# Hybrid encoder trunk: early loads at the FFN entry, and three layer boundaries interleaved by input chunk

## The chip, the cores and the metric

The kernel runs on one core of one Trainium2 chip (trn2). The metric is the device time of one execution in microseconds (us); lower is better. The profile is one execution's, taken by the hardware profiler.

## The reference

Two layers over a sequence of 256 tokens of width 2048, all float32. Each half of a layer is a sandwich of RMS norms around a matrix chain:

```
for layer in range(2):
    h = rms_norm(x, norm_mix_pre[layer])
    m = even_mixer(h, ...) if layer == 0 else diff_attention_mixer(h, ...)
    x = x + rms_norm(m, norm_mix_post[layer])
    h = rms_norm(x, norm_ffn_pre[layer])
    f = (silu(h @ w_gate) * (h @ w_up)) @ w_down          # 2048 -> 5632 -> 2048
    x = x + rms_norm(f, norm_ffn_post[layer])
```

The mixers are one input projection (2048 to 5120 in layer 0, 2048 to 6144 in layer 1), recurrence and attention, and one output projection (2048 to 2048).

## The kernel before, in words

**Products.** Every weight matrix is cut into 512x512 pieces of 1 MB, the "units" u = 0, 1, 2 ... in the order of use. SP loads a piece into a raw buffer (L775). ACT writes its float32r rounding, `w_hi` (L909, task `hi`). DVE writes the remainder, `w_lo = raw - w_hi` (L1499, task `lo`), which also sets the raw buffer free. PE multiplies in three passes, w_hi with the high part of the activations, w_lo with the high part, w_hi with their low part (L1241), for 128 tokens at a time: a `half(slot, t)` is 12 matmuls, t is 0 or 1. There are four `w_hi` buffers and three `w_lo` buffers, so `hi(u)` waits until PE has done unit u-4 and `lo(u)` until it has done u-3. There are five raw buffers. Three (`raw`) serve the mixers and boundaries; two more (`gx`, `queries`) belong to the attention and serve as raw buffers 3 and 4 in the FFN blocks only.

**Order.** Nothing is scheduled at run time. One list of tasks per part is written out beforehand and every engine goes through it in order, doing its own share of each task and waiting on semaphores. So a task that waits holds back all that stands behind it on its engine.

**Boundaries.** Between two matrix chains (b=1: mixer output of layer 0 to FFN of layer 0, b=2: FFN of layer 0 to mixer of layer 1, b=3: mixer to FFN of layer 1) stands `boundary(b, before, after)`, an order written out by hand. `before` are the last four units (column groups s0 to s3 of the old output); for each column group and token half there are: add_output (DVE L1579), y_square (ACT L925), rms_y (DVE, then POOL), y_gain (POOL or DVE L1571), update of the residual (DVE L1562), `turn` (four PE transposes L1264, then high part by ACT L955 and low part by DVE L1537), square (ACT L925). When all squares of the new residual are there, rms_x gives the scale of the next norm (POOL). `after` are the first four units of the next chain, e, f, g, h: one column group over the four 512-wide chunks of the input, chunk by chunk. `head_end` lists the rest of the FFN's head.

**FFN.** The first 512 of the 5632 columns are the "head": four gate units, then four up units, silu (ACT L1107) and gate_up (DVE L1773). The other ten pieces of columns are "blocks" (class Body). A block saves matmuls: the products of the 2x2 corner of input chunks 0 and 1, token halves 0 and 1, gate and up, are made from seven products (P1 to P7) of sums and differences of weights and activations instead of eight. `ENTRIES` is the order of PE, `LOADS` that of SP. P1 needs g0; P5 the difference u0-g0, formed on DVE in g0's buffer (L1512); P3 needs u1; P6 u1 minus that difference (L1514), P7 u1-u0 (L1517), P4 g1 minus what g0's buffer then holds (L1519). The activations' sums S1 to S4 ("left sums") are made once per layer: eight additions on POOL (L1980 to L1996), then high parts (ACT L1118) and low parts (DVE L1528). P5 needs S1, P3 needs S4. The blocks' products P1 to P7 are at L1254. After P5, PE transposes gate_up's result for the down products.

**Buffers of the loads.** `place_loads` goes through the loads in SP's order and gives each the buffer whose last load is oldest by a number `age`; the load waits until what was in that buffer is released. In a block u1's buffer is released by form P7, u0's by lo P7, g0's by lo P4, g2's by lo g2, g1's by form P4. In the kernel before, the block's loads are u1, u0, g0, g2, g1, and then u3 takes u1's buffer, g3 u0's, u2 g0's, and so on in rotation. Ahead of the first block SP issues the gain vector of the next norm, 1 MB as it lands (L817), then these loads.

The DVE's order in a block, which the prediction follows, begins:

```
form(body, "P6"); low("P3"); low("P6"); low("g2"); form(body, "P7"); second()
low("P2"); form(body, "P4"); low("P7"); low("P4"); low("u3"); third()
```

Of the kernel before, what the change touches and what calls it, by code (L numbers as in the profile page):

```python
# [59 lines left out]
KEYS_SLOT = ((20, 31), (4,))  # L60
# [38 lines left out]
LOADS = ("u1", "u0", "g0", "g2", "g1", "u3", "g3", "u2", "d0", "d1", "d3", "d2")  # L99
FORMS = ("P5", "P6", "P7", "P4")  # L100
# [4 lines left out]
class Body:  # L105


    def __init__(self, layer, j, index, u, n, e, m, n_head):

        self.layer, self.j, self.index, self.first = layer, j, index, j == 0  # L110
        self.base, self.e, self.m = u, e, m
        self.u = {name: u + i for i, name in enumerate(ENTRIES)}
        self.up, self.gate, self.down = n, n + 1, n + 2
        self.head_up, self.next = n_head + 1, None
        self.form = {name: len(FORMS) * index + i + 1 for i, name in enumerate(FORMS)}
        self.sum = {name: len(SUMS) * index + i + 1 for i, name in enumerate(SUMS)}

# [39 lines left out]
def mixer_slots(plan, layer):  # L157
# [7 lines left out]
    if layer == 0:  # L165
        order = ([("xr", g, 2 + g) for g in range(2)] + [("gate", g, g) for g in range(2)]
                 + [(w, g, 4 + 2 * i + g) for g in range(2) for i, w in enumerate("qkv")])
        groups, w_in, w_out = 2, "ev_in", "ev_out"
    else:
        order = [(w, g, 4 * i + g) for g in range(4) for i, w in enumerate("qkv")]  # L170
        groups, w_in, w_out = 4, "od_in", "od_out"
# [6 lines left out]
    if layer == 0:  # L178
        for kg in range(NC):
            for _, g, cb in order[:2]:  # L180
                slots.append(plan.slot(w_in, kg, plan.n + g, kg == 0, kg == NC - 1, cb=cb, region="h", layer=layer))
        plan.n += 2
    for i, (what, g, cb) in enumerate(order):
        if layer == 0 and i < 2:
# [25 lines left out]
    starts = [evacs["v", g].s + 1 + 2 * (layer == 0 and g == 0) for g in range(groups)]  # L210
    for s in range(len(slots)):
        for kind, lag in (("s0", 0), ("pt", 1), ("pv", 2), ("s", 0)):
            for g, start in enumerate(starts):
                i = s - start - lag
                if 0 <= i < HEADS_OF_GROUP:
                    task = put(s, kind=kind, g=g, i=i, n=plan.heads + HEADS_OF_GROUP * g + i, v_group=evacs["v", g].n)
                    if kind == "pt" and layer == 1:
                        slots[s].early.append(Task("difference", n=task.n))
# [75 lines left out]
def head_end(slots, body):  # L294

    def left(name):
        return Task("sums", 2 * body.layer + 1, body.layer, what=name)

    tasks = []
    for i, s in enumerate(slots):  # L300
        last = len(slots) - 1 - i
        tasks += half(s, 0)
        tasks += [hi(u) for u in range(ahead(s.u - 1, HI_LEAD), min(ahead(s.u, HI_LEAD), body.base + 1))]
        tasks += [lo(u) for u in range(ahead(s.u - 1, LO_LEAD), min(ahead(s.u, LO_LEAD), body.base + 1))]
        if last == 1:
            tasks += [Task("form", src=body, what="P5"), hi(body.base + 1), lo(body.base + 1)]
        if last == 0:
            tasks += [left("S1"), left("S3")]
        tasks += half(s, 1) + s.post
    return tasks + [left("S2"), left("S4")]  # L310
# [35 lines left out]
def boundary(b, before, after):  # L346


    update, turn, square = boundary_tasks(b)
    add, y_square, rms_y, y_gain = y_tasks(b)  # L350
    s0, s1, s2, s3 = before
    e, f, g, h = after
    u = s0.u
    tasks = [hi(u + 3)] + half(s0, 0) + [lo(u + 2)] + half(s1, 0) + half(s0, 1, [add(s1, 0), add(s0, 0)])
    tasks += [hi(u + 4), y_square(s1, 0)] + half(s2, 0, [lo(u + 3)]) + [add(s2, 0), y_square(s0, 0), add(s0, 1)]
    tasks += half(s1, 1) + half(s3, 0)
    tasks += [add(s1, 1), lo(u + 4), y_square(s2, 0), y_gain(1, 0), y_square(s0, 1), add(s3, 0), y_square(s1, 1), y_gain(0, 0), y_gain(1, 1, "dve"), y_gain(0, 1, "dve")]
    tasks += half(s2, 1, [y_square(s3, 0)]) + [rms_y(0), add(s2, 1), update(0, 0), hi(u + 5), y_square(s2, 1)]
    tasks += half(s3, 1)
    tasks += [update(1, 0), lo(u + 5), add(s3, 1), turn(0, 0), y_square(s3, 1), y_gain(2, 1), y_gain(2, 0), rms_y(1), turn(1, 0)]  # L360
    tasks += half(e, 0)
    tasks += half(f, 0, [update(0, 1), update(2, 0), hi(u + 6)], [y_gain(3, 0, "dve"), update(1, 1), turn(0, 1), square(0, 0)])
    tasks += [turn(1, 1)] + half(e, 1, [square(1, 1)])
    tasks += [update(2, 1), lo(u + 6), update(3, 0), hi(u + 7), y_gain(3, 1, "dve"), turn(2, 0), turn(2, 1), update(3, 1)]
    tasks += half(f, 1, [square(2, 0), lo(u + 7), square(2, 1)], [hi(u + 8)]) + half(g, 0, [square(1, 0)])
    tasks += [turn(3, 0), square(3, 0)] + half(g, 1)
    tasks += [turn(3, 1), square(0, 1), hi(u + 9), square(3, 1), hi(u + 10)] + half(h, 0) + [lo(u + 8)]
    tasks += half(h, 1, [Task("rms_x", b), *h.post]) + [lo(u + 9)]
    return tasks
# [82 lines left out]
def make_plan():  # L452
    plan, before = Plan(), None
    for layer in range(2):
# [4 lines left out]
                for w, n in (("gate", n_gate), ("up", n_up)) for kg in range(NC)]  # L459
# [3 lines left out]
        head[NC - 1].post.append(Task("silu", 2 * layer + 1, n=n_gate, u=head[NC - 1].u))  # L463
# [8 lines left out]
        n_start = NC if before else 2 * NC  # L472
        start = boundary(2 * layer, before, slots[:NC]) if before else first_boundary(slots[:n_start])
        tasks = (start + run(slots[n_start:-NC]) + boundary(2 * layer + 1, slots[-NC:], head[:NC]) + head_end(head[NC:], bodies[0]))
# [30 lines left out]
def place_loads(plan):  # L505
# [4 lines left out]
    def take(key, buffers, released):  # L510
# [6 lines left out]
        age[buf] = BLOCK_RAW + order  # L517

    age[3:] = [-2, -1]
    for part in plan.parts:  # L520
        for task in part.tasks or ():
            if task.kind == "tile_unit" or task.kind == "half" and task.t == 0 and task.passes[0] == 0:
                take(task.slot.u, range(RAW), (("lo", task.slot.u + 1),))
        for body in part.bodies or ():
            lo_of = {name: ("lo", u + 1) for name, u in body.u.items()}
            form_of = {name: ("form", n) for name, n in body.form.items()}
            released = {"g0": (lo_of["P4"],), "u0": (lo_of["P7"],), "u1": (lo_of["P3"], form_of["P7"]),
                        "g1": (lo_of["P2"], form_of["P4"])}
            for name in LOADS:
                take((body.index, name), range(BLOCK_RAW), released.get(name) or (lo_of[name],))  # L530
# [7 lines left out]
def trunk(nc, x, norm_mix_pre, norm_mix_post, norm_ffn_pre, norm_ffn_post,  # L538
# [9 lines left out]
    with ExitStack() as ctx:  # L548
# [215 lines left out]
        def _(sp):  # L764
# [53 lines left out]

            def load_slot(slot):
# [8 lines left out]
            def task_of(task):  # L828
                if task.kind == "tile_unit" or task.kind == "half" and task.t == 0 and task.passes[0] == 0:
                    load_slot(task.slot)  # L830
                elif task.kind == "gains":
# [22 lines left out]
            for part in plan.parts:  # L854
# [4 lines left out]
                wg, wu, wd = (weights[w][part.layer] for w in ("gate", "up", "down"))  # L859

                def block_load(body, name):

                    cols, rows = slice((body.j + 1) * KC, (body.j + 2) * KC), slice(body.j * KC, (body.j + 1) * KC)
                    k = int(name[1])
                    if name[0] == "d":
                        src = wd[rows, k * KC:(k + 1) * KC]
                    else:
                        src = (wg if name[0] == "g" else wu)[k * KC:(k + 1) * KC, cols]
                    load((body.index, name), src)

                sp.wait_ge(s_done, plan.heads_of[part.layer])
                for body in part.bodies:
                    for name in LOADS:
# [324 lines left out]
        def _(pe):  # L1198
# [59 lines left out]

            def transposes(e, pieces):
# [10 lines left out]
            def task_of(task):  # L1270
# [13 lines left out]
                elif task.kind == "T":  # L1284
# [19 lines left out]
                    else:  # L1304
                        transposes(task.e, quarter(task.e, src, task.t))
                elif task.kind == "tile_unit":
# [71 lines left out]
            for part in plan.parts:  # L1378
# [10 lines left out]
                def rows(kg, t):  # L1389
                    return [b[:, kg * KT:(kg + 1) * KT, t * P:(t + 1) * P] for b in (h_hi, h_lo)]  # L1390

# [25 lines left out]

                def down(body, j):
# [5 lines left out]
                def block(body):  # L1424
# [10 lines left out]
                    for name in ENTRIES:  # L1435
                        if name == "P1":
                            if not body.first:
                                pe.wait_ge(copied[0], body.index)
                            formed(body, name, product1, rows(0, 0), True, True)
# [612 lines left out]
```

## Time and profile before

| | us |
|---|---|
| median of 3 runs | 2233.23 |
| lowest, highest | 2232.08, 2234.36 |
| profiled execution, its time | 2234.35 |
| its span in the trace | 2232.6 |
| PE busy in it | 2202.4 (99%) |
| DVE, ACT, POOL busy | 1688.6, 1176.9, 309.9 |
| mean granted TensorE clock | 0.997 |

PE is TensorE's matmul side, PEld its weight loads, DVE VectorE, ACT ScalarE, POOL GpSimd, SP the engine that issues the transfers. The times of a timeline count from the start of the span. A busy PE is a stretch covered by matmuls; what it is short of the span is time in which no matmul ran. "<- X" names what released a waiting instruction. The three boundaries lie around 356 to 410, 1071 to 1125 and 1486 to 1540 us. The first blocks of the two layers begin at 427 and 1557 us.

### The profile page before, as it was taken

What the parts mean: (1) busy time and instruction counts of PE and PEld (TensorE: products, weight loads), DVE (VectorE), ACT (ScalarE), POOL (GpSimd) and SP (SyncE); (2) the same over time, 40 slices, a digit from 0 to 9 for tenths busy, and PEclk for the clock granted to TensorE, in tenths of its full rate; (3) what the DMA queues carried; (4) which work ended last, traced back from release to release, by engine and by line L of the source; (5) the groups of instructions that cost most, each with busy time, mean ns of one, the idle gap of its engine ahead of it and who ended that gap; (6) DMA issues with size and microseconds to landing.
All of it is one profiled execution on the core that took longest, in us unless ns stands there. A gap on an engine that the chain in (4) does not pass through costs nothing.

```text
span 2232.6 us, 26301 instructions
## 1 busy us (share of the span) xinstructions
PE 2202.4 (99%) x10011; PEld 1812.0 (81%) x10011; DVE 1688.6 (76%) x1680; ACT 1176.9 (53%) x1330; POOL 309.9 (14%) x253
## 2 busy tenths in 40 slices
PE   8999999999999999999999999999999999999998
PEld 6888888788888888888787888787788888888886
DVE  5587467788888888888746555777888888888886
ACT  6677545545554444454655555546454444444543
POOL 0851001200000000000121001003000000000001
PEclk9999999999999999999999999999999999999999
DMA  8545444466564445664564545455565445565543
GB/s 306 184 162 172 167 132 151 170 226 226 189 225 174 172 171 205 222 226 152 177 214 137 170 151 169 170 169 191 196 219 186 173 171 204 208 226 204 211 170 113
DMA packets 213883, 416.52 MB, mean 187 GB/s; under 512 B 12328, under 2 KB 14976, under 8 KB 213248
## 3 DMA queue, kind: packets, MB, share of 16 engines
q1 hardware_dynamic: 213040, 414.29, 53.0%
q8 instruction: 81, 1.33, 0.2%
q10 hardware_dynamic: 720, 0.56, 0.1%
q14 instruction: 42, 0.34, 0.0%
HBM read 412.73 MB, written 2.10 MB: 186 GB/s over the span
## 4 chain that ended last, share of the span: by engine, by line
PE 92%; DVE 3%; DMA 2%; issue 1%; ACT 1%; SPq 1%; ACTq 0%; POOLq 0%; POOL 0%; DVEq 0%
PE acc L1241 69%; PE acc L1254 12%; PE tp L1264 2%; PE sc L1254 2%; PE pv L1254 2%; DMA raw<-in_ffn_w_gate 1%; PE sc L1344 1%; DVE w_lo L1499 1%; PE pv L1373 1%; PE sc L1340 1%; DMA raw<-in_ev_w_in 1%; PE pv L1368 1%; ACT w_hi L909 0%; DMA yacc<-in_x_T 0%; PE sc L1323 0%
## 5 line engine op out<-in xcount | busy, mean ns | idle before, releaser
L909 ACT ACTIVATE w_hi<-raw 128x2048 fp32r<-128x2048 f32 x321 | 612.9, 1915 | 454.8 <-DVE raw L1512 93.4
L1499 DVE TENSOR_TENSOR w_lo<-raw,w_hi 128x2048 fp32r<-128x2048 f32 x321 | 735.8, 2303 | 134.8 <-ACT w_hi L909 92.3
L1241 PE MATMUL acc<-w_hi,h_hi 128*128 128x512 f32 x1576 | 431.5, 396 | 4.4 <-ACT h_hi L955 2.7
L1241 PE MATMUL acc<-w_hi,h_lo 128*128 128x512 f32 x1576 | 423.3, 390 | 1.6 <-DVE h_lo L1537 1.4
L1241 PE MATMUL acc<-w_lo,h_hi 128*128 128x512 f32 x1576 | 422.6, 390 | 1.1 <-DVE w_lo L1499 1.1
L1241 PEld LDWEIGHTS acc<-w_hi,h_lo 128*128 128x128 f32 x1576 | 295.9, 188 | 64.9 <-DVE h_lo L1537 2.7
L1241 PEld LDWEIGHTS acc<-w_lo,h_hi 128*128 128x128 f32 x1576 | 296.0, 188 | 64.1 <-DVE w_lo L1499 1.6
L1241 PEld LDWEIGHTS acc<-w_hi,h_hi 128*128 128x128 f32 x1576 | 291.1, 188 | 64.6 <-issue 6.7
L1241 PE MATMUL acc<-w_hi,y_hi 128*128 128x512 f32 x832 | 224.5, 392 | 0.7 <-ACT y_hi L1113 0.7
L1241 PE MATMUL acc<-w_lo,y_hi 128*128 128x512 f32 x832 | 222.6, 389 | 0.0
L1241 PE MATMUL acc<-w_hi,y_lo 128*128 128x512 f32 x832 | 222.5, 389 | 0.0
L2002 POOL TENSOR_TENSOR probT<-probT,rgx 128x512 f32<-128x512 f32 x20 | 40.8, 2040 | 1143.0 <-ACT rgx L1148 1143.0
L1579 DVE TENSOR_TENSOR yacc<-acc,yacc 128x512 f32<-128x512 f32 x208 | 138.7, 686 | 76.0 <-PE acc L1241 76.0
L1241 PEld LDWEIGHTS acc<-w_lo,y_hi 128*128 128x128 f32 x832 | 156.2, 188 | 32.7
L1241 PEld LDWEIGHTS acc<-w_hi,y_lo 128*128 128x128 f32 x832 | 156.2, 188 | 32.5
L1241 PEld LDWEIGHTS acc<-w_hi,y_hi 128*128 128x128 f32 x832 | 155.1, 188 | 32.9 <-issue 1.6
L909 ACT ACTIVATE w_hi<-queries 128x2048 fp32r<-128x2048 f32 x60 | 115.0, 1916 | 122.3 <-DVE queries L1512 34.6
L909 ACT ACTIVATE w_hi<-gx 128x2048 fp32r<-128x2048 f32 x60 | 114.9, 1916 | 121.4 <-DVE gx L1512 34.7
L1499 DVE TENSOR_TENSOR w_lo<-gx,w_hi 128x2048 fp32r<-128x2048 f32 x60 | 137.2, 2286 | 17.1 <-ACT w_hi L909 17.1
L1499 DVE TENSOR_TENSOR w_lo<-queries,w_hi 128x2048 fp32r<-128x2048 f32 x60 | 137.2, 2286 | 16.1 <-ACT w_hi L909 16.1
L1254 PE MATMUL acc<-w_hi,lefts 128*128 128x512 f32 x320 | 88.6, 399 | 0.0
L1016 ACT ACTIVATE probT<-tp 128x256 f32<-128x256 f32 (+1 forms) x48 | 22.0, 457 | 114.6 <-PE pv L1373 65.0
(250 smaller groups left out, 2315.6 us busy)
## 6 DMA issues: line engine op xcount, KB each, us to landing
raw<-in_ffn_w_gate SPq DMA_DIRECT2D x56, 1024.0 KB, 5.3
raw<-in_ffn_w_up SPq DMA_DIRECT2D x56, 1024.0 KB, 6.7
raw<-in_ffn_w_down SPq DMA_DIRECT2D x56, 1024.0 KB, 10.3
raw<-in_od_w_in SPq DMA_DIRECT2D x48, 1024.0 KB, 5.1
raw<-in_ev_w_in SPq DMA_DIRECT2D x37, 1024.0 KB, 5.2
raw<-in_ev_w_out SPq DMA_DIRECT2D x16, 1024.0 KB, 5.1
gx<-in_ffn_w_up SPq DMA_DIRECT2D x16, 1024.0 KB, 7.0
queries<-in_ffn_w_up SPq DMA_DIRECT2D x16, 1024.0 KB, 7.2
```

The costliest lines, as they stand in the source:

```text
L909: act.activation(w_hi[u % HI][:, :, :], raw[place.buf][:, :, :], ACT.Copy).then_inc(hi_done, 1)
L1016: act.activation(flat_pt[:, 0:cols], flat_tp[:, 0:cols], ACT.Copy).then_inc(tp_free[task.e % 2], 1)
L1241: mm = pe.matmul(acc[n % 2][t][:, :], operand(lhs, a, k, t), w[:, k, :], start=first and k == 0 and j == 0, stop=last and k == KT - 1 and ...
L1254: mm = pe.matmul(bank, a[:, k, :], w[:, k, :], start=start and k == 0 and j == 0, stop=stop and k == KT - 1 and j == 2)
L1264: ins = pe.transpose(dst, src, ident[:, :])
L1340: mm = pe.matmul(sc[:, t, :], q[:, kt, t * P:(t + 1) * P], k[:, kt, task.i % 2, :], start=True, stop=True)
L1344: mm = pe.matmul(sc[:, :, :].rearrange("p m t -> p (m t)"), q[:, kt, t * P:(t + 1) * P], k[:, kt, :, :].rearrange("p m t -> p (m t)"), sta ...
L1368: mm = pe.matmul(pv[:, 0, t * HD:(t + 1) * HD], probT[:, j, t * P:(t + 1) * P], v[:, j, task.i * HD:(task.i + 1) * HD], start=j == 0, stop ...
L1373: mm = pe.matmul(pv[:, 0, 0:CV], flat_pt[:, j * P:(j + 1) * P], v[:, j, hd * CV:(hd + 1) * CV], start=j == 0, stop=j == 1)
L1499: dve.tensor_tensor(w_lo[u % LO][:, :, :], raw[plan.place[u].buf][:, :, :], w_hi[u % HI][:, :, :].bitcast(F32), ALU.subtract).then_inc(lo_ ...
L1579: dve.tensor_tensor(y, a, y, ALU.add).then_inc(acc_free[n % 2][t], 1)
L2002: pool.tensor_tensor(spare[1], spare[1], spare[3], ALU.add).then_inc(spread, 1)
```

## The change

It has four parts.

1. **Boundaries.** `boundary` gets six units after it instead of four, a0 to a5. They are two column groups (gate and up in the head, q and v in layer 1's mixer) interleaved by input chunk: a0, a1 use chunk 0, a2, a3 chunk 1, a4, a5 chunk 2. Its written-out order is new. Layer 1's mixer has the order q, v, k in its first group, its attention starts two units later, and the clearing of the keys moves from slot 4 to 6.
2. **P1 in the head.** The first product P1 of a layer's first block moves between the last two units of the head; it takes the number of the head's last unit, which moves up by one. All four left sums are listed in the last unit but one, ahead of form P5, hi P5, lo P5, which are listed in the last unit (before: form P5 in the last but one, S1 and S3 in the last, S2 and S4 behind it).
3. **Early loads.** g0 and u0 of the first block are loaded ahead of the head's last two units, into buffers 3 and 4, with 3.5 added to their `age`. The first block's loads are then u1, g2, g1, u3, g3, u2, ...
4. SP's wait for the heads (`s_done`) goes with the early loads. The rest is code that is moved.

```diff
-KEYS_SLOT = ((20, 31), (4,))
+KEYS_SLOT = ((20, 31), (6,))
+EARLY = ("g0", "u0")
+EARLY_LEAD = 3.5
...
+        if self.first:
+            self.u["P1"] = u - 1
...
+def loads_of(body):
+    return tuple(name for name in LOADS if not (body.first and name in EARLY))
...
-        order = [(w, g, 4 * i + g) for g in range(4) for i, w in enumerate("qkv")]
+        columns = {"q": 0, "k": 4, "v": 8}
+        order = [(w, g, columns[w] + g) for g in range(4) for w in ("qkv" if g else "qvk")]
...
+    for kg in range(NC):
+        for i, (_, _, cb) in enumerate(order[:2]):
+            slots.append(plan.slot(w_in, kg, plan.n + i, kg == 0, kg == NC - 1, cb=cb, region="h", layer=layer))
+    plan.n += 2
...
+    if layer == 1:
+        starts[0] = evacs["k", 0].s + 3
...
+    def ahead_of(slot, before, lead):
+        return range(ahead(before, lead), min(ahead(slot.u, lead), body.u["P5"]))
+    tasks, before = [], slots[0].u - 1
     for i, s in enumerate(slots):
+        if i == 0:
+            tasks += [Task("early_load", src=body, what=name) for name in EARLY]
+        if i == len(slots) - 1:
+            tasks.append(Task("first_product", src=body))
         tasks += half(s, 0)
+        tasks += [hi(u) for u in ahead_of(s, before, HI_LEAD)] + [lo(u) for u in ahead_of(s, before, LO_LEAD)]
+        before = s.u
+        if i == len(slots) - 2:
+            tasks += [left("S1"), left("S3"), left("S2"), left("S4")]
+        if i == len(slots) - 1:
+            tasks += [Task("form", src=body, what="P5"), hi(body.u["P5"]), lo(body.u["P5"])]
         tasks += half(s, 1) + s.post
...
+    a0, a1, a2, a3, a4, a5 = after
     u = s0.u
+    tasks = half(s0, 0, [hi(u + 3)]) + half(s0, 1) + half(s1, 0, [lo(u + 2)], [hi(u + 4), add(s0, 1)])
+    tasks += half(s1, 1, [], [lo(u + 3)]) + [add(s1, 0), y_square(s1, 0), hi(u + 5), add(s0, 0)] + half(s2, 0)
+    tasks += [y_gain(1, 0, "dve"), lo(u + 4), add(s2, 0)] + half(s3, 0, [y_square(s0, 0)], [y_gain(0, 0, "dve")])
+    tasks += [y_square(s2, 0), add(s3, 0), y_square(s3, 0), y_gain(2, 0), rms_y(0)] + half(s2, 1, [], [add(s1, 1)])
+    tasks += [y_square(s0, 1), update(0, 0), add(s2, 1), hi(u + 6), lo(u + 5)]
+    tasks += half(s3, 1, [turn(0, 0), y_square(s1, 1)])
+    tasks += [add(s3, 1), update(1, 0), y_gain(0, 1, "dve"), y_gain(1, 1), y_square(s2, 1), y_square(s3, 1), rms_y(1), update(0, 1)]
+    tasks += half(a0, 0) + [lo(u + 6), turn(1, 0)] + half(a1, 0, [], [turn(0, 1), y_gain(3, 1, "dve")])
+    tasks += half(a2, 0) + [update(1, 1), hi(u + 7)] + half(a0, 1)
+    tasks += [update(2, 0), square(2, 0), hi(u + 8), y_gain(3, 0, "dve"), lo(u + 7), square(0, 1), update(3, 0), y_gain(2, 1, "dve"), update(2, 1), turn(2, 0), square(1, 0)]
+    tasks += half(a1, 1) + half(a3, 0, [turn(1, 1)]) + [hi(u + 9), turn(2, 1), square(1, 1), update(3, 1)]
+    tasks += half(a2, 1) + half(a3, 1, [hi(u + 10)]) + [lo(u + 8), turn(3, 0), lo(u + 9)] + half(a4, 0)
+    tasks += [hi(u + 11), lo(u + 10), turn(3, 1), lo(u + 11), square(0, 0), hi(u + 12)] + half(a4, 1)
+    tasks += half(a5, 0, [], [square(2, 1)]) + [square(3, 1)] + half(a5, 1) + [square(3, 0), Task("rms_x", b)]
...
         head = [plan.slot(w, kg, n, kg == 0, kg == NC - 1, layer=layer)
-                for w, n in (("gate", n_gate), ("up", n_up)) for kg in range(NC)]
+                for kg in range(NC) for w, n in (("gate", n_gate), ("up", n_up))]
+        head[-1].u += 1
...
-    def take(key, buffers, released):
+    def take(key, buffers, released, later=0):
...
-        age[buf] = BLOCK_RAW + order
+        age[buf] = BLOCK_RAW + order + later
...
-            if task.kind == "tile_unit" or task.kind == "half" and task.t == 0 and task.passes[0] == 0:
+            if task.kind == "early_load":
+                take((task.src.index, task.what), range(RAW, BLOCK_RAW), released(task.src, task.what), EARLY_LEAD)
+            elif task.kind == "tile_unit" or task.kind == "half" and task.t == 0 and task.passes[0] == 0:
...
+                elif task.kind == "early_load":
+                    if task.what == EARLY[0]:
+                        sp.wait_ge(s_done, plan.heads_of[task.src.layer])
+                    block_load(task.src, task.what)
...
-                sp.wait_ge(s_done, plan.heads_of[part.layer])
                 for body in part.bodies:
-                    for name in LOADS:
+                    for name in loads_of(body):
                         block_load(body, name)
...
+            def first_product(body):
+                single(body.u["P1"], product1, *rows(0, 0), True, True)
```

## Rows read from the trace of the kernel before

**Rows 1.** The page, part 1: busy us, share of the span, instructions of each engine

```profile
PE 2202.4 (99%) x10011; PEld 1812.0 (81%) x10011; DVE 1688.6 (76%) x1680; ACT 1176.9 (53%) x1330; POOL 309.9 (14%) x253
```

**Rows 2.** Windows: stretch; its us, PE, PEld, DVE, ACT, POOL busy (count), PEclk, DMA, GB/s

```profile
370.00:460.00 90.00, 83.36 (x382) 67.70 (x381) 72.25 (x83) 53.12 (x83) 22.31 (x13) 1.00 0.47 164
...
1085.00:1120.00 35.00, 33.65 (x162) 27.39 (x161) 32.01 (x60) 26.27 (x62) 6.13 (x5) 1.00 0.41 135
...
1500.00:1590.00 90.00, 84.79 (x383) 68.94 (x382) 72.47 (x83) 53.86 (x83) 22.31 (x13) 0.98 0.49 170
```

**Rows 3.** Waits of PE, whole span: us in total, times, longest us

```profile
PE acc L1254 <- DVE w_lo L1499: 5.4, 2, 2.7
PE pv L1254 <- DVE y_lo L1528: 3.7, 2, 2.6
PE acc L1241 <- ACT h_hi L955: 2.7, 3, 0.9
...
PE acc L1241 <- DVE h_lo L1537: 1.4, 3, 0.5
```

**Rows 4.** Chain that ended last, 370 to 450 us: start, us, what

```profile
391.05 5.46 PE acc L1241 x24
...
407.00 14.28 DMA raw<-in_ffn_w_gate
```

**Rows 5.** Timeline of DVE: start, us, line, operation, [idle before <- releaser]

```profile
375.98 1.41 DVE L1562 SCALAR_TENSOR_TENSOR xs<-yacc,small,xs 128x512 f32<-128x512 f32 x2
...
429.74 2.29 DVE L1499 TENSOR_TENSOR w_lo<-raw,w_hi 128x2048 fp32r<-128x2048 f32 x1 [1.98 <-ACT w_hi L909]
...
433.15 1.40 DVE L1773 SCALAR_TENSOR_TENSOR tok<-acc,small,stage 128x512 f32<-128x512 f32 x2
...
435.67 2.28 DVE L1514 TENSOR_TENSOR raw<-gx,raw 128x2048 f32<-128x2048 f32 x1
...
437.87 2.28 DVE L1499 TENSOR_TENSOR w_lo<-gx,w_hi 128x2048 fp32r<-128x2048 f32 x1
...
456.09 2.28 DVE L1499 TENSOR_TENSOR w_lo<-gx,w_hi 128x2048 fp32r<-128x2048 f32 x1
```

**Rows 6.** Timeline of ACT, the same columns

```profile
378.54 0.63 ACT L955 ACTIVATE h_hi<-tp,pre 128x128 fp32r<-128x128 f32 x2 [1.65 <-PE sc L1264]
...
403.65 0.64 ACT L925 ACTIVATE junk<-xs 128x512 bf16<-128x512 f32 x1
...
427.79 1.92 ACT L909 ACTIVATE w_hi<-raw 128x2048 fp32r<-128x2048 f32 x1 [4.56 <-DVE raw L1512]
...
453.63 1.90 ACT L909 ACTIVATE w_hi<-gx 128x2048 fp32r<-128x2048 f32 x1
```

**Rows 7.** Timeline of POOL, the same columns: the left sums

```profile
407.50 2.83 POOL L1980 TENSOR_TENSOR probT<-h_hi,h_lo 128x512 f32<-128x512 f32 x1
...
411.66 3.22 POOL L1987 TENSOR_TENSOR prob<-prob,probT 128x512 f32<-128x512 f32 x1
...
414.84 1.29 POOL L1980 TENSOR_TENSOR rgx<-h_hi,h_lo 128x512 f32<-128x512 f32 x1
...
420.19 1.29 POOL L1996 TENSOR_TENSOR probT<-probT,rgx 128x512 f32<-128x512 f32 x1
```

**Rows 8.** Timeline of PE, entry of the first block of layer 0

```profile
432.68 1.19 PE L1254 MATMUL pv<-w_hi,y_hi 128*128 128x512 f32 x4 [2.56 <-DVE y_lo L1528]
...
440.21 1.20 PE L1254 MATMUL acc<-w_lo,lefts 128*128 128x512 f32 x4 [2.70 <-DVE w_lo L1499]
...
458.73 1.07 PE L1241 MATMUL acc<-w_hi,h_hi 128*128 128x512 f32 x4
```

**Rows 9.** Timeline of SP, 427 to 475 us: the load of u3

```profile
446.84 0.37 SPq L775 DMA_DIRECT2D gx<-in_ffn_w_up  x1
```

**Rows 10.** DMA issues, 404 to 414 us and 452 to 458 us: issue to landing

```profile
raw<-in_ffn_w_up SPq DMA_DIRECT2D x1, 1024.0 KB, 5.2
...
raw<-in_ffn_w_up SPq DMA_DIRECT2D x1, 1024.0 KB, 6.3
```

**Rows 11.** Windows of 2.5 us, PEclk the third column from the end

```profile
1567.50:1570.00 2.50, 1.06 (x3) 0.87 (x4) 2.50 (x2) 2.50 (x2) 0.00 (x0) 0.70 0.00 0
```

More of the change, by code:

```diff
@@ L176, in put @@
         return task
[L178 to L182, printed above, removed]
+    for kg in range(NC):
+        for i, (_, _, cb) in enumerate(order[:2]):
+            slots.append(plan.slot(w_in, kg, plan.n + i, kg == 0, kg == NC - 1, cb=cb, region="h", layer=layer))
+    plan.n += 2
     for i, (what, g, cb) in enumerate(order):
-        if layer == 0 and i < 2:
+        if i < 2:
             s = len(slots) - 2 + i
@@ L297, in left @@
         return Task("sums", 2 * body.layer + 1, body.layer, what=name)
-    tasks = []
+    def ahead_of(slot, before, lead):
+        return range(ahead(before, lead), min(ahead(slot.u, lead), body.u["P5"]))
+    tasks, before = [], slots[0].u - 1
     for i, s in enumerate(slots):
-        last = len(slots) - 1 - i
+        if i == 0:
+            tasks += [Task("early_load", src=body, what=name) for name in EARLY]
+        if i == len(slots) - 1:
+            tasks.append(Task("first_product", src=body))
         tasks += half(s, 0)
[L303 to L308, printed above, removed]
+        tasks += [hi(u) for u in ahead_of(s, before, HI_LEAD)] + [lo(u) for u in ahead_of(s, before, LO_LEAD)]
[4 more added lines that the diff above has]
+            tasks += [Task("form", src=body, what="P5"), hi(body.u["P5"]), lo(body.u["P5"])]
         tasks += half(s, 1) + s.post
-    return tasks + [left("S2"), left("S4")]
+    return tasks
 def boundary_tasks(b):
@@ L351, in boundary @@
     s0, s1, s2, s3 = before
-    e, f, g, h = after
+    a0, a1, a2, a3, a4, a5 = after
     u = s0.u
[L354 to L368, printed above, removed]
+    tasks = half(s0, 0, [hi(u + 3)]) + half(s0, 1) + half(s1, 0, [lo(u + 2)], [hi(u + 4), add(s0, 1)])
+    tasks += half(s1, 1, [], [lo(u + 3)]) + [add(s1, 0), y_square(s1, 0), hi(u + 5), add(s0, 0)] + half(s2, 0)
@@ L462, in make_plan @@
                 slot.b = b
-        head[NC - 1].post.append(Task("silu", 2 * layer + 1, n=n_gate, u=head[NC - 1].u))
+        head[-2].post.append(Task("silu", 2 * layer + 1, n=n_gate, u=head[-2].u))
         head[-1].post += [Task("gate_up", n=n_gate, u=head[-1].u), Task("gains", 2 * layer + 2)]
@@ L471, in make_plan @@
         plan.n += 6 * NF
-        n_start = NC if before else 2 * NC
-        start = boundary(2 * layer, before, slots[:NC]) if before else first_boundary(slots[:n_start])
-        tasks = (start + run(slots[n_start:-NC]) + boundary(2 * layer + 1, slots[-NC:], head[:NC]) + head_end(head[NC:], bodies[0]))
+        n_start = 2 * NC - 2 if before else 2 * NC
+        start = boundary(2 * layer, before, slots[:n_start]) if before else first_boundary(slots[:n_start])
+        tasks = (start + run(slots[n_start:-NC]) + boundary(2 * layer + 1, slots[-NC:], head[:-2]) + head_end(head[-2:], bodies[0]))
         number(plan, tasks)
@@ L516, in take, with released @@
         order += 1
-        age[buf] = BLOCK_RAW + order
+        age[buf] = BLOCK_RAW + order + later
+    def released(body, name):
+        lo_of = {entry: ("lo", u + 1) for entry, u in body.u.items()}
+        form_of = {entry: ("form", n) for entry, n in body.form.items()}
+        return {"g0": (lo_of["P4"],), "u0": (lo_of["P7"],), "u1": (lo_of["P3"], form_of["P7"]),
+                "g1": (lo_of["P2"], form_of["P4"])}.get(name) or (lo_of[name],)
     age[3:] = [-2, -1]
@@ L521, in place_loads @@
         for task in part.tasks or ():
-            if task.kind == "tile_unit" or task.kind == "half" and task.t == 0 and task.passes[0] == 0:
+            if task.kind == "early_load":
+                take((task.src.index, task.what), range(RAW, BLOCK_RAW), released(task.src, task.what), EARLY_LEAD)
+            elif task.kind == "tile_unit" or task.kind == "half" and task.t == 0 and task.passes[0] == 0:
                 take(task.slot.u, range(RAW), (("lo", task.slot.u + 1),))
         for body in part.bodies or ():
[L525 to L528, printed above, removed]
-            for name in LOADS:
-                take((body.index, name), range(BLOCK_RAW), released.get(name) or (lo_of[name],))
+            for name in loads_of(body):
+                take((body.index, name), range(BLOCK_RAW), released(body, name))
             for name in FORMS:
@@ L817, in gains, with block_load @@
                 sp.dma_start(post_gain, post.partition_broadcast(P)).then_inc(gain_in, 16)
+            def block_load(body, name):
+                cols, rows = slice((body.j + 1) * KC, (body.j + 2) * KC), slice(body.j * KC, (body.j + 1) * KC)
+                k = int(name[1])
+                if name[0] == "d":
+                    src = weights["down"][body.layer][rows, k * KC:(k + 1) * KC]
+                else:
+                    src = weights["gate" if name[0] == "g" else "up"][body.layer][k * KC:(k + 1) * KC, cols]
+                load((body.index, name), src)
             def load_slot(slot):
@@ L858, in _ @@
                     continue
[L859 to L869, printed above, removed]
-                sp.wait_ge(s_done, plan.heads_of[part.layer])
                 for body in part.bodies:
-                    for name in LOADS:
+                    for name in loads_of(body):
                         block_load(body, name)
@@ L1257, in single, with rows @@
                 mm.then_inc(unit_done, 1)
+            def rows(kg, t):
+                return [b[:, kg * KT:(kg + 1) * KT, t * P:(t + 1) * P] for b in (h_hi, h_lo)]
+            def first_product(body):
+                single(body.u["P1"], product1, *rows(0, 0), True, True)
             def transposes(e, pieces):
@@ L1305, in task_of @@
                         transposes(task.e, quarter(task.e, src, task.t))
+                elif task.kind == "first_product":
+                    first_product(task.src)
                 elif task.kind == "tile_unit":
@@ L1387, in down_operand @@
                     transposes(e + t, quarter(e + t, tok, t))
-                def rows(kg, t):
-                    return [b[:, kg * KT:(kg + 1) * KT, t * P:(t + 1) * P] for b in (h_hi, h_lo)]
                 def open_bank(body, name, column, t):
@@ L1438, in block @@
                                 pe.wait_ge(copied[0], body.index)
-                            formed(body, name, product1, rows(0, 0), True, True)
+                                first_product(body)
                         elif name == "P5":
```

## The prediction

> **What bounds the kernel.** I read the page first: PE is busy 2202.4 of 2232.6 us [rows 1], so the change can win only from the 30.2 us in which no matmul runs, and can lose whatever it adds to them. It adds and removes no matmul. Then the windows by stage [rows 2]: PE is idle 6.64 us around the first boundary and the entry of layer 0's blocks, 1.35 us at the second boundary, 5.21 us around the third: 13.20 us. The rest is the start and the end of the kernel, which stay as they are. The list of PE's waits [rows 3] says what the 13.2 us are. Each boundary has a wait of 0.9 for the first high part of the new residual and of 0.5 for its low part, 4.1 us in all three. The two FFN entries have 3.7 us (P5 waiting for the left sum S1) and 5.4 us (P3 waiting for its w_lo), 9.1 us in all.
>
> The chain [rows 4] shows where the entry's first wait comes from: P1's weight g0 is the last of a burst of loads and lands 14.28 us after its issue. Everything else of the entry (form P5, hi P5, lo P5, the left sums' parts, gate_up, form P6, lo P3) stands behind it in DVE's and ACT's order. The wait for P3 is DVE's own work: from the end of lo P5 to the end of lo P3 it is busy without a gap [rows 5].
>
> **The boundaries.** The first turn needs update(0,0). Before, it stands on DVE behind the add of s2's second token half, together with update(1,0), at 375.98 [rows 5], and PE transposes only when s3 is done. Then it waits for the high part, which ACT begins at 378.54 [rows 6]. After, update(0,0) stands ahead of that add, and the turn sits inside s3's last half with two passes, 1.8 us, behind it to hide ACT's high part (two pairs of 0.63, [rows 6]). Chunk 1 is needed two units after chunk 0 starts instead of one, so each later turn has more room: a unit is 5.46 us [rows 4]. Following the queues through, the narrow places are the add of s1's second half ahead of s3's second half, update(0,1) ahead of its turn and the low part of chunk 1, each within some 0.3 us of PE. I leave 0.2 us per boundary: 3 x (1.37 - 0.2) = -3.5 us. Bounds: all gone, -4.1; unchanged, 0; one DVE operation late at each of the three, +2.2 x 3 (a w_lo, [rows 5]). I take -3.5, nearest to the count of the queue.
>
> **Early g0 and u0** land before ACT gets to them: SP issues them behind the load of a5, more than a unit ahead of hi P1. P1 ceases to wait, and so does the burst. That removes the cause of the first entry wait.
>
> **The left sums take its place.** Let Z be the time at which PE ends a5 and begins the head's last unit but one. rms_x stands behind square(3,0) in ACT's order, and this behind hi of the head's last unit, which waits until PE has done a4, at Z - 5.5. 1.9 for the hi, three squares of 0.64 plus their read-outs [rows 6], the mean and POOL's power end about at Z. Only then does POOL begin the left sums. Before, they ran from 407.50 to 421.48 [rows 7], 14.0 us, of which the first and third lost 1.5 and 1.9 to two w_lo beside them (2.83 and 3.22 for what is 1.29 elsewhere). After, one w_lo of 2.2 lies beside them: 14.0 - 3.5 + 2.2 = 12.7, so S4 is there at Z + 12.7, its high and low part at Z + 14.0. Before, that was some 6 us ahead of PE's need; but now form P5 stands behind S4's low part on DVE. Form 2.2, hi P5 1.9 [rows 6], lo P5 2.2: Z + 20.4. PE has two units and P1, 5.5 + 2.7 + 5.5, and P5's first pass 0.9 to do: Z + 14.5. **P5 waits 5.9 us.** Then DVE has gate_up 1.3, form P6 2.2, lo P3 2.2 = 5.7 us [rows 5]. PE wanted lo P3 before at 440.21 - 2.70 = 437.51, that is 4.8 after P5's start and 3.9 after P5's second pass [rows 8]: **P3 waits 1.9 us**. An entry costs 7.8 us where it cost 5.3 in layer 0 and 3.9 in layer 1: +2.5 + 3.9 = +6.4 us. Bounds per entry: 1.9 (left sums early) and 9.7. The upper one holds POOL also for the low parts of S1, S3 and S2.
>
> The trace shows POOL's additions held only by w_lo [rows 7], never by a low part of a left sum. The Trainium skill, GPSIMD Engine Reference, section 1 (Specifications), says that GpSimd shares its SBUF interfaces with VectorE and contends with any DVE instruction that has two SBUF inputs. The low parts are such instructions, so by it the upper bound would hold (some 1.9 us later), and by the row alone the 7.8.
>
> **u3 loses its early buffer.** With 3.5 on their ages, g0 and u0 stand at k + 3.5 and k + 4.5 where the head's last two units are k + 2 and k + 3 and u1, g2, g1 are k + 4, 5, 6. So u1, g2, g1 go to the three raw buffers, and the oldest after them is g0's, not u1's. u3's load therefore waits for the release of g0's buffer, lo P4, instead of form P7. Before it was issued at 446.84 [rows 9]; lo P4 ends where lo u3 begins, 456.09 [rows 5]. hi u3 was done at 453.63 + 1.90 [rows 6] and lo u3 at 458.3, PE began u3 at 458.73 [rows 8] and its second pass at 459.6: only 1.3 us to spare. After: issue at 456.2, 5.2 us to land (the first load of a burst, [rows 10]), hi 1.9, lo 2.2: 465.5. **u3 waits 5.9 us.** The times hold against the end of lo P3, from which DVE is busy without a gap and from which PE runs, before and after. Twice, once a layer: +11.8 us. Bounds: 5.9, and 7.0 with the 6.3 us of the load that had others around it [rows 10]; 0 if I have the ages wrong. g3, behind u3, lands before PE has done u3.
>
> **The clock.** In the third entry, layer 1's, the granted clock fell to 0.70 in one window of 2.5 us [rows 11] after the waits of 1.2 and 2.7, and in layer 0's it did not (means 0.98 and 1.00 [rows 2]): part of that window was at the lower level, 1.2 GHz, the rest at 2.4. 0.3 x 2.5 and as much again behind it make 1.5 us. After, there are four longer waits (entry and u3, twice) and the low level covers partly the next wait. I take 1.5 more than one such drop in all, +2.2 in sum; bounds -1.5 and +6.
>
> **Costed at nothing:** the order q, v, k in layer 1's mixer and its attention two units later (PE has other units beside it, and no wait of rows 3 lies there; if a group's end met the next one's start, a wait of 1 to 2 us would show); P1's move; the keys' clearing on POOL; SP's wait.
>
> **Sum.** -3.5 + 6.4 + 11.8 + 2.2 = +16.9. The profiled span 2232.6 becomes 2249.5, its execution's 2234.35 becomes 2251.2. The median shown, 2233.23, is 1.1 below that execution: 2250.
>
> **Rivals.** About 0.2% (4.5 us) is what a measurement can tell from no change.
> 1. *Only u3 is late* (0.14). If POOL finishes 6 us earlier than I count, each entry has P3's 1.9 alone: -3.5 - 5.3 + 11.8 + 1 = +4, 2237. For it: POOL alone takes 1.29 an addition. Against: they can't begin before rms_x.
> 2. *Faster* (0.08). The late g0 was all that was wrong: left sums as in 1, and u3's load hidden. It decides at its landing: 453.6 or so against my 461.4. Price -3.5 - 5.3 = -8.8, 2224. For it: rows 3 name nothing else. Against: 1.3 us to spare.
> 3. *The loads share* (0.06). u3, g3, u2, d0, d1 are all free to go at lo P4's end. If they shared the rate, u3 would land 9 us later, like g0's 14.28 [rows 4]: +18, 2268. Against: the first of the burst at 404 landed in 5.2 with others right behind it. The Trainium skill, DMA: Bandwidth & Descriptors, Queues, rings and completion order, says that completion is not FIFO per issuing engine, which leaves this open.
> 4. *The boundaries wait too* (0.08): the narrow places fail by a w_lo each, some +6: 2256.
>
> The forecast has the remaining 0.64, with a range of its own of 2242 to 2258. The range over the cases, 2236 to 2262, leaves out rivals 2 and 3. Slower by over 0.2%: the forecast, 3, 4 and part of 1, 0.82. Within: most of the rest of 1, 0.09. Faster 0.09.
>
> **What would show it.** In the profile after: no wait for h_hi or h_lo over 0.3 at the boundaries; hi P1 not released by a transfer; PE waiting some 6 us around P5 for hi and lo, with DVE idle behind S4's high part; POOL's left sums beginning at the end of a5; u3's issue released by lo P4 and PE waiting 4.6 for its hi and 1.3 for its lo. I am wrong if u3's load is issued ahead of lo P4, or if form P5 ends before PE has ended the head.

## The result and the profile after

| | before | after |
|---|---|---|
| median, us | 2233.36 (4 runs) | 2248.77 (4 runs) |
| lowest, highest | 2232.08, 2234.36 | 2248.48, 2250.24 |
| profiled execution | 2234.35 | 2248.48 |
| its span | 2232.6 | 2246.7 |

The ratio is 1.0070, 95% interval 1.0055 to 1.0085: 15.4 us slower, where 16.8 (2250 against 2233.23) were forecast. The page's first part after, to be read beside [rows 1]:

```profile
PE 2208.9 (98%) x10011; PEld 1814.7 (81%) x10011; DVE 1693.9 (75%) x1686; ACT 1179.4 (52%) x1330; POOL 288.7 (13%) x247
```

The same 10011 matmuls are there. PE's idle time rose from 30.2 to 37.8 us, and its busy time by 6.5 us, which no added work explains. The second is for the most part the clock, below. PE's longest waits after, over the whole span (us in total, times, longest), answer to [rows 3]:

```profile
PE pv L1276 <- ACT w_hi L931: 11.1, 2, 5.6
PE acc L1263 <- ACT w_hi L931: 9.1, 2, 4.6
PE acc L1263 <- ACT h_hi L903: 2.0, 1, 2.0
PE acc L1225 <- POOL gq L1996: 1.5, 1, 1.5
PE acc L1263 <- DVE w_lo L1527: 1.3, 3, 0.6
PE acc L1276 <- DVE w_lo L1527: 1.0, 1, 1.0
```

The waits for h_hi and h_lo of the boundaries are gone (the one for h_hi L903 is in the first 50 us). In their place and in that of the entries' two waits stand 5.6 us at P5 and 4.6 us at u3, once per layer. The windows after show the second boundary without any idle time, where [rows 2] had 1.35 us (columns as there):

```profile
1080.00:1120.00 40.00, 40.00 (x188) 32.72 (x188) 31.38 (x51) 24.68 (x51) 3.69 (x4) 1.00 0.49 159
```

**The entry of layer 0.** Timelines of POOL, ACT and DVE, merged by time; PE ends a5 at 411.5, which is the prediction's Z, and wants P5 at 425.25:

```profile
411.49 1.29 POOL L2008 TENSOR_TENSOR probT<-h_hi,h_lo 128x512 f32<-128x512 f32 x1
...
411.76 3.17 DVE L1527 TENSOR_TENSOR w_lo<-raw,w_hi 128x2048 fp32r<-128x2048 f32 x1 [1.01 <-PE acc L1263]
...
412.74 3.34 POOL L2008 TENSOR_TENSOR prob<-h_hi,h_lo 128x512 f32<-128x512 f32 x1
...
422.45 1.55 DVE L1556 TENSOR_TENSOR y_lo<-rgx,y_hi 128x512 fp32r<-128x512 f32 x1 [0.15 <-ACT y_hi L1140]
...
423.53 1.62 POOL L2024 TENSOR_TENSOR probT<-probT,rgx 128x512 f32<-128x512 f32 x1
...
426.45 2.29 DVE L1540 TENSOR_TENSOR gx<-queries,gx 128x2048 f32<-128x2048 f32 x1
...
430.71 2.29 DVE L1527 TENSOR_TENSOR w_lo<-gx,w_hi 128x2048 fp32r<-128x2048 f32 x1 [1.98 <-ACT w_hi L931]
```

The left sums begin at Z exactly, S4 is there at 425.15 (Z + 13.65, 12.7 forecast), form P5 begins behind S4's low part at 426.45, lo P5 ends at 432.9. PE in the same stretch and at u3 (a group is four matmuls; [] is the idle time before it and its releaser):

```profile
430.82 2.05 PE L1276 MATMUL pv<-w_hi,y_hi 128*128 128x512 f32 x4 [5.57 <-ACT w_hi L931]
...
433.06 2.07 PE L1276 MATMUL pv<-w_lo,y_hi 128*128 128x512 f32 x4 [0.19 <-DVE w_lo L1527]
...
438.78 1.19 PE L1276 MATMUL acc<-w_lo,lefts 128*128 128x512 f32 x4
...
462.03 2.08 PE L1263 MATMUL acc<-w_hi,h_hi 128*128 128x512 f32 x4 [4.57 <-ACT w_hi L931]
...
464.35 2.08 PE L1263 MATMUL acc<-w_lo,h_hi 128*128 128x512 f32 x4 [0.25 <-DVE w_lo L1527]
...
467.79 1.08 PE L1263 MATMUL acc<-w_hi,h_hi 128*128 128x512 f32 x4
```

**u3.** Its load is issued when lo P4 is done, and lands in 5.3 us although four more loads are issued right behind it (timeline of SP; DMA issues of 450 to 470 us, issue to landing):

```profile
454.76 0.37 SPq L796 DMA_DIRECT2D gx<-in_ffn_w_up  x1
```

```profile
gx<-in_ffn_w_up SPq DMA_DIRECT2D x1, 1024.0 KB, 5.3
```

**The clock.** Groups of four that take 1.07 to 1.2 us elsewhere take 2.05 to 2.08 behind both waits. The windows of these stretches (PEclk is the third column from the end):

```profile
427.50:430.00 2.50, 0.00 (x0) 0.00 (x0) 1.24 (x1) 2.12 (x3) 0.00 (x0) 1.00 0.00 0
430.00:432.50 2.50, 1.68 (x4) 1.16 (x4) 1.79 (x1) 2.48 (x2) 0.00 (x0) 0.51 0.00 0
...
462.50:465.00 2.50, 2.25 (x6) 1.24 (x6) 2.50 (x3) 1.91 (x1) 0.00 (x0) 0.50 1.05 388
```

0.50 is 1.2 GHz instead of 2.4. The engine had been idle for 5.57 and 4.57 us before.

**Where the time went,** from like points in the two traces. From the time PE wants P5 to P3's second pass: 430.12 to 440.21 before [rows 8], 425.25 to 438.78 after, +3.4 us; in layer 1 +4.8. From there to u3's second token half: 21.2 us before, 29.0 after, +7.8; in layer 1 +5.6 (less, since there the kernel before lost 1.3 us of clock at this place [rows 11]). The three boundaries gave back 1.7, 1.0 and 1.7 us, 4.4 in all, of which 4.1 are their waits: PE comes to the first entry 4.9 us earlier than before (3.1 of them from the start, see below) and to the first u3's second half 6.4 later, reaches the third boundary 5.4 later and wants P5 in layer 1 3.7 later (1560.25 and 1563.94).

What is left of the difference lies in the first 50 us. The transposes at 54.98 before stand at 51.85 after, 3.1 us earlier, although the change leaves this code as it is. In the run below of the kernel before with one number changed, whose start is the same code too, they stand at 52.38. So the trace before had a slow start: its granted clock over the first 50 us is 0.97 (1.00 after), and PE's waits there add up to 6.5 us, 4.7 after and 3.8 to 5.7 in the eight experiments. The sum of the parts is then 3.4 + 7.8 + 4.8 + 5.6 - 4.4 - 3.1 = 14.1, the difference of the two spans.

### The profile page after: what moved, and what is told of

Read it like the earlier page. It is cut to its first block, busy times and chain, and to the rows that moved or that the text cites. A ratio compares the mean times of both kernels' runs of the same rounds, so it can differ in the third digit from the quotient of the medians.

```text
span 2246.7 us, 26301 instructions
## 1 busy us (share of the span) xinstructions
PE 2208.9 (98%) x10011; PEld 1814.7 (81%) x10011; DVE 1693.9 (75%) x1686; ACT 1179.4 (52%) x1330; POOL 288.7 (13%) x247
## 4 chain that ended last, share of the span: by engine, by line
PE 88%; issue 4%; DVE 3%; POOL 1%; DMA 1%; ACT 1%; SPq 1%; POOLq 0%; DVEq 0%; ACTq 0%
PE acc L1263 67%; PE acc L1276 11%; PE tp L1292 2%; PE sc L1276 2%; PE pv L1276 2%; DVE w_lo L1527 1%; PE sc L1374 1%; DMA raw<-in_ev_w_in 1%; PE pv L1403 1%; PE sc L1370 1%; ACT w_hi L931 1%; PE pv L1398 1%; DMA gx<-in_ffn_w_up 0%; PE sc L1353 0%; PE pv L1353 0%
## 5 line engine op out<-in xcount | busy, mean ns | idle before, releaser
L931 ACT ACTIVATE w_hi<-gx 128x2048 fp32r<-128x2048 f32 x66 | 126.5, 1917 | 154.6 <-DVE gx L1540 35.0
L1527 DVE TENSOR_TENSOR w_lo<-gx,w_hi 128x2048 fp32r<-128x2048 f32 x66 | 150.9, 2287 | 35.1 <-ACT w_hi L931 35.1
L931 ACT ACTIVATE w_hi<-queries 128x2048 fp32r<-128x2048 f32 x54 | 103.4, 1916 | 84.8 <-DVE queries L1540 17.5
L1527 DVE TENSOR_TENSOR w_lo<-queries,w_hi 128x2048 fp32r<-128x2048 f32 x54 | 123.5, 2286 | 14.0 <-ACT w_hi L931 14.0
```

Source lines behind the costliest of these rows:

```text
L931: act.activation(w_hi[u % HI][:, :, :], raw[place.buf][:, :, :], ACT.Copy).then_inc(hi_done, 1)
L1527: dve.tensor_tensor(w_lo[u % LO][:, :, :], raw[plan.place[u].buf][:, :, :], w_hi[u % HI][:, :, :].bitcast(F32), ALU.subtract).then_inc(lo_ ...
```

## The experiments

Times are medians, ratios are to the kernel before, which ran beside each set: 2232.6 us in both. The first four runs take apart the two losses.

**Age.** The early loads' ages alone:

```diff
-EARLY_LEAD = 3.5
+EARLY_LEAD = 5.5
```

> The changed kernel with 5.5 instead of 3.5 on the ages of g0 and u0, so that u3 goes to u1's buffer again and nothing else is moved. Theory (u3 waits for its load because g0's buffer comes free late): PE's 4.6 and 0.3 us ahead of u3 go in both first blocks, and with them the stretch at the lower clock behind them, 2.5 to 3 us each: 2248.8 - 15 = 2234. Rival (DVE and ACT are late at u3 anyway, from the late entry, and the load only looked like the cause): at most 3 us in all, 2246 or more, with PE waiting for w_hi or w_lo of u3 that no transfer releases.

Measured 2234.4 us (ratio to before 1.0009, 1.0000 to 1.0018): 14.4 us less than the change. PE no longer waits for u3's w_hi or w_lo, and the waits at P5 are the same 5.6 us. So the buffer is a cause by itself, and worth 7.2 us a layer on average, wait and clock together.

**Form P5 first.** The two lines of the last unit but one and of the last become one:

```diff
         if i == len(slots) - 2:
+            tasks += [Task("form", src=body, what="P5"), hi(body.u["P5"]), lo(body.u["P5"])]
             tasks += [left("S1"), left("S3"), left("S2"), left("S4")]
-        if i == len(slots) - 1:
-            tasks += [Task("form", src=body, what="P5"), hi(body.u["P5"]), lo(body.u["P5"])]
```

> The changed kernel with form P5, hi P5 and lo P5 ahead of the four left sums in the head's last unit but one; buffers as changed. Theory (P5 waits because form P5 stands behind S4's parts): the 5.6 us ahead of P5 and the lower clock behind them go, but POOL is now held by form P5 too, S4 comes some 2 us later and gate_up, form P6 and lo P3 stand behind it, so P3 waits 2 to 4 us: 4 to 6 us less per entry, 2248.8 - 10 = 2239. Rival (VectorE has too much work there, in whatever order): P3 or P5 waits as long as before, 2247 or more.

Measured 2249.1 us (1.0077, 1.0061 to 1.0092), 10 us above my expectation: nothing won in the median (the profiled execution, from which the lines come, was the fastest of four, 2245.6). The wait moved. PE's longest waits, and one of POOL's additions:

```profile
PE tp L1291 <- DVE tok L1800: 9.2, 2, 4.6
PE acc L1262 <- ACT w_hi L930: 6.6, 2, 3.3
PE acc L1275 <- DVE w_lo L1526: 2.8, 2, 1.4
```

```profile
416.54 3.23 POOL L2014 TENSOR_TENSOR prob<-prob,probT 128x512 f32<-128x512 f32 x1
```

P5 starts on time, but form P5 and lo P5 now lie beside POOL's additions and hold them; S4 comes 4 us later. Behind its high part on ACT stands silu, behind silu gate_up on DVE, and PE waits 4.6 us for the transposes of gate_up's result. I had followed DVE's queue and forgotten silu in ACT's. What the rival said, that no order within the head helps, holds for this one order; others were not tried. The next run looks further up, at when the sums begin.

**Sums early.** POOL starts them in the boundary, ACT's and DVE's parts stay:

```diff
     tasks += half(a1, 1) + half(a3, 0, [turn(1, 1)]) + [hi(u + 9), turn(2, 1), square(1, 1), update(3, 1)]
+    if b % 2:
+        tasks += [Task("pool_sums", b, b // 2)]
...
-                elif task.kind == "sums" and task.what == LEFT[0]:
+                elif task.kind == "pool_sums":
```

> The changed kernel with POOL's eight left-sum additions begun within the boundary, as soon as input chunks 0 and 1 are turned, ahead of rms_x; ACT's and DVE's parts of the left sums stay where they are. Theory (the sums start late because they stand behind rms_x on POOL): no wait at P5, P3 waits 1 to 2 us, 7 us less per entry; the w_lo and updates in the boundary are held by POOL and may cost up to 1.5 us at each of the two FFN boundaries: 2248.8 - 14 = 2235, up to 2238. Rival (hi P5 is late for another reason, ACT's table load and silu or the transfer): 2247 or more, P5 still waiting for w_hi.

Measured 2233.4 us (1.0005, 0.9996 to 1.0014), 15.4 us less than the change. No wait at P5 is left, P3's are two of 0.7 us. The price is small: a w_lo in the boundary takes 3.38 us beside an addition, and PE waits for none there.

**Both.**

> The edits of e1 and e3 together. Theory (two causes, independent, both on PE's path): the gains add, 2248.8 - 15 - 14 = 2220, some 13 us under the kernel before the change; what is left is a wait of 1 to 2 us at P3 in each entry. Rival (DVE's work becomes the bound once either is gone, so that the gains overlap): 2228 or more.

Measured 2218.2 us (0.9938, 0.9925 to 0.9950). The gains add: 14.4 + 15.4 = 29.8, measured 30.6 under the change, and 14.4 under the kernel before. The granted clock of the profiled execution is 0.998. PE's waits but those of the first 50 us and three of 0.3 or less:

```profile
PE acc L1278 <- DVE w_lo L1529: 1.4, 2, 0.7
```

The next four ran on another chip, on the base of this kernel, of the kernel before, or of the change. What compares them with the runs above is the ratio.

**P3's work ahead of gate_up,** on the kernel with both:

```diff
             tasks += [Task("form", src=body, what="P5"), hi(body.u["P5"]), lo(body.u["P5"])]
+            tasks += [hi(body.u["P3"]), Task("form", src=body, what="P6"), lo(body.u["P3"])]
```

(and the first block leaves these three out of its own lists)

> e4, and in the first block of each layer hi P3, form P6 and lo P3 stand ahead of gate_up in the head's last unit instead of behind it. Theory (the 0.7 us that PE still waits at P3 is DVE's form P6 and lo P3 queued behind gate_up, which waits for PE): both waits of 0.7 go, 2218.2 - 1.4 = 2217, with no wait left at the entries. Rival (gate_up becomes late and PE waits at the transposes of its result): 2218 or more, with a wait of PE for DVE tok.

Measured 2217.3 us (0.9934, 0.9921 to 0.9946). Both waits of 0.7 are gone and two of 0.3 for gate_up's result are new. 0.9 less, in the expected direction and inside both intervals: no more than a hint in the times. In the trace the move of the waits is clear. It has the lowest time of all that ran, 15 us under the kernel before.

**u3's buffer in the kernel before.** Only the age of g0 in each first block:

```diff
-                take((body.index, name), range(BLOCK_RAW), released.get(name) or (lo_of[name],))
+                take((body.index, name), range(BLOCK_RAW), released.get(name) or (lo_of[name],),
+                     -2.5 if body.first and name == "g0" else 0)
```

> The kernel before the change with one number added: -2.5 on the age of g0 in the first block of each layer, so that u3 takes g0's buffer (released by lo P4) and all else stays. Theory: u3's load is issued some 9 us later, PE waits 4.6 us for its hi and 0.2 to 1.3 for its lo, and then has 1.7 us of lower clock, 6.4 to 7 us a layer: 2232.6 + 13 = 2246. Rival (what was lost is not the buffer but the order of the head): within 2 us of the kernel before.

Measured 2246.7 us (1.0065, 1.0052 to 1.0079), 14.1 us slower than before. This one number does nearly what the whole change did. The new waits:

```profile
PE acc L1242 <- ACT w_hi L910: 9.1, 2, 4.6
```

**Filler.** In the change, matmuls without use inside the two waits:

```diff
+FILL = (22, 18)
...
+                            if body.first:
+                                filler(product5, FILL[0])
                             formed(body, name, product5, None, True, True)
...
+                            if name == "u3" and body.first:
+                                pe.wait_ge(copied[0], body.index + 1)
+                                filler(product1, FILL[1])
```

> The changed kernel, and in each first block 22 matmuls on data that is already there, into P5's bank ahead of P5's wait, and 18 into P1's copied bank ahead of u3's wait (4.7 and 3.9 us at full clock, inside waits of 5.6 and 4.6); their results are used nowhere. Theory (the lower clock behind a wait costs time only where nothing else is waited for): the granted clock stays at 2.4 GHz in both places; at the entries nothing is won, since P3's w_lo ends at the same time and PE then waits 1.9 us for it; behind u3 1.7 us are won, twice: 2248.8 - 3.4 = 2245.4. Rival (the lower clock at the entries is on the path too): 2243 or less. Rival (the clock doesn't depend on the wait): 2248.8.

Measured 2247.4 us (1.0068, 1.0053 to 1.0084): 1.4 less, 3.4 expected, and the spans of the two profiled executions differ by 1.8. At the entries nothing is won, as expected. In layer 0 this is no clean test, since the clock fell again behind the filler (the passes of P5 take 1.17, 1.95 and 1.91 us): P3's second pass starts at 438.85, 438.78 in the change. In layer 1 all of P5 runs at full clock (1.17, 1.19 and 1.08 us, where the change has 2.04, 2.00 and 1.09), and PE waits 1.81 us for P3's w_lo instead of 0.99:

```profile
1568.08 1.17 PE L1277 MATMUL pv<-w_hi,y_hi 128*128 128x512 f32 x4 [0.60 <-ACT w_hi L932]
1570.32 1.19 PE L1277 MATMUL pv<-w_lo,y_hi 128*128 128x512 f32 x4 [1.07 <-DVE w_lo L1538]
...
1576.04 1.50 PE L1277 MATMUL acc<-w_lo,lefts 128*128 128x512 f32 x4 [1.81 <-DVE w_lo L1538]
```

From the last real group ahead of P5 to this pass it is 14.61 us, 14.59 in the change: the wait took back all that the clock gave. At u3 the engine runs at full clock:

```profile
462.07 1.20 PE L1264 MATMUL acc<-w_hi,h_hi 128*128 128x512 f32 x4 [0.46 <-ACT w_hi L932]
464.40 1.19 PE L1264 MATMUL acc<-w_lo,h_hi 128*128 128x512 f32 x4 [1.13 <-DVE w_lo L1538]
...
466.35 1.08 PE L1264 MATMUL acc<-w_hi,h_hi 128*128 128x512 f32 x4
```

The second token half begins 4.28 us after the first pass, 5.76 in the change: 1.5 us won in this layer. In layer 1 the change has 4.86 us there (1600.64 to 1605.50), so that only 0.6 is to be won; from P3's second pass to u3's second token half it is 27.7 us with the filler and 28.0 in the change, 0.4 won. The expectation took layer 0's loss, and a little more, twice. The two traces give 1.9 in all, near the median's 1.4 and the spans' 1.8.

**The turn put back,** in the kernel with both:

```diff
-    tasks += [y_square(s0, 1), update(0, 0), add(s2, 1), hi(u + 6), lo(u + 5)]
-    tasks += half(s3, 1, [turn(0, 0), y_square(s1, 1)])
+    tasks += [y_square(s0, 1), add(s2, 1), update(0, 0), hi(u + 6), lo(u + 5)]
+    tasks += half(s3, 1, [y_square(s1, 1)]) + [turn(0, 0)]
```

> e4 with two things of the new boundary order put back in all three boundaries: update(0,0) behind the add of s2's second half, and the turn of (0,0) behind s3's last half instead of inside it. Theory (the 0.9 and 0.5 us at each boundary came from these two, the interleaving by chunk only gives the later turns room): PE waits again 0.9 for the first high part and 0.1 to 0.5 for the low part, 1.0 to 1.4 x 3: 2218.2 + 3 to 4 = 2221.7. Rival (the interleaving removed them): 2219 or less.

Measured 2222.7 us (0.9956, 0.9943 to 0.9968), 4.5 us more by the medians and 4.0 by the ratios, with

```profile
PE acc L1265 <- ACT h_hi L979: 4.0, 3, 1.3
```

So the boundary's gain hangs on these two places; they were put back together, and what each is worth by itself is open. The interleaving by chunk doesn't remove this wait; that it gives the later turns room was not tried by itself.

## Why the prediction was right

- **Boundaries,** -3.5 us: right in place, 0.9 too small. All 4.1 us of waits went, 4.4 us by like points, and no narrow place failed. The order of layer 1's mixer, costed at nothing, lies in the second boundary's 1.0, which is 0.4 short of that boundary's waits; no run takes it apart.
- **Early g0 and u0:** right. hi P1 starts at 401.28 straight behind ACT's instruction ahead of it and waits for no transfer.
- **The left sums behind rms_x, form P5 behind S4:** right in mechanism, shown by the run that starts the sums early. The waits' sizes: P5 5.57 + 0.19 where 5.9 were forecast, P3 0 and 1.0 where 1.9 were. The entries cost 3.4 and 4.8 us more than before, 8.2 in all against 6.4. The missing 1.8 us is the hold that I put into the upper bound only: S1, S3 and S2's low parts on DVE and POOL's additions slow each other (1.55 for a low part that takes 0.68 where POOL is idle, 1.62 for an addition's 1.29 [rows 7]), and S4 comes 0.95 later than forecast. That no row before showed such a hold said nothing: there the additions end at 421.48 and the first low part begins at 431.95, so that none could meet. The Trainium skill, GPSIMD Engine Reference, section 1 (Specifications), speaks of contention with any VectorE instruction that has two SBUF inputs; by that rule I should have added it. The trace agrees, at 0.95 us an entry, half the 1.9 that I gave for its full weight. (PE's need of lo P3 was 3.8 us after P5's second pass by [rows 8], not 3.9; the forecast 1.9 goes by the 3.8.)
- **u3:** right. Issue at lo P4's end, 5.3 us to land, 4.57 + 0.25 us of wait in layer 0. The wait is shorter than the forecast 5.9 because the first pass, at the lower clock, filled most of the 1.3 us ahead of the second; the first token half then takes 5.76 us (462.03 to 467.79) instead of the 2.72 of twelve matmuls at full clock. By like points and without the clock the waits at u3 cost 6.3 and 6.2 us, 12.5 where 11.8 were forecast. Age and buffer are shown twice, by undoing it in the change and doing it in the kernel before.
- **The clock,** +2.2 us: right to be there, too large. It fell in all four places. Where P3's w_lo is waited for anyway it costs nothing; behind u3 it costs 1.5 us in layer 0 and 0.6 in layer 1, and the 1.3 us that the kernel before lost in layer 1 are gone: +0.8 in all. The forecast named the cover by the next wait, but sized it too small. With the wait, u3 costs 7.8 and 5.6 us, 13.4 in all, against 11.8 + 2.2 = 14.0.
- **Sum:** by like points +8.2 + 13.4 less 4.4, 17.2, against 16.9. The profiled executions differ by 14.1, the first 50 us having been 3.1 us shorter in the one after. The medians differ by 15.4. The entries came out 1.8 us above their term and the waits at u3 0.7, the clock 1.4 and the boundaries 0.9 below theirs. The causes are right; that the sum is this close is chance.
- **Rivals:** u3 alone late (2237) is what the sums-early run gave in substance (2233.4). The faster case needed both causes gone: 2218. The loads did not share: the first of five landed in 5.3 us.

## What to carry to other kernels

When a transfer is moved to remove a wait, look at what its buffer was released by, and who had that buffer next: one number in an allocation order cost 14 us here, by a load issued some 9 us later in each layer. A task list hides long chains over four engines (rms_x, POOL's sums, DVE's parts, the next weight): follow the queue of every engine to what stands behind, not only the wait that is named. Start slow side work when its inputs are ready, not where its result is consumed; moving only the consumer left the time as it was.

## What the runs showed of the hardware

- After idle stretches of 4.6 and 5.6 us PE ran at 1.2 GHz, granted 0.50, through two or three groups of four matmuls. A lower clock behind a wait hides the next wait, so its cost can't be read from the slow matmuls alone: in layer 1's entry the filler brought P5's passes back to full clock, and PE waited that much longer for P3's weight.
- Filling the wait with 22 matmuls kept the clock at 1.00 up to 433 us, and yet it fell for a stretch right behind, with waits of only 0.6 and 1.1 us in between; in layer 1 it held there and fell behind a further wait of 1.81, to 0.50 in the last window below. In layer 0 of the kernel before it held through waits of 2.56 and 2.70 [rows 8]. So the length of a wait alone doesn't decide it; what does stays open:

```profile
430.00:433.00 3.00, 1.47 (x6) 0.67 (x4) 2.22 (x2) 2.55 (x2) 0.00 (x0) 1.00 0.00 0
433.00:436.00 3.00, 2.87 (x7) 2.30 (x8) 3.00 (x4) 0.00 (x0) 0.00 (x0) 0.55 0.03 5
...
1577.50:1580.00 2.50, 2.50 (x8) 1.93 (x7) 2.50 (x2) 2.50 (x5) 0.00 (x0) 0.50 0.02 7
```

- POOL's additions and DVE's two-operand instructions on SBUF hold each other up, as if they took turns: the one that begins second ends later by about what the first still had to go. The w_lo begun at 411.76, 1.02 us ahead of an addition's end, took 3.17 instead of 2.28; the addition begun at 412.74, 2.19 ahead of that w_lo's end, took 3.34 instead of 1.29; the low part begun at 422.45, 1.00 ahead of an addition's end (421.70 + 1.75), took 1.55 instead of 0.68.
